# Out-projection products and gated sums of the prompt tiles placed inside the sample-attention loop

## The reference, cut to what matters

```python
def merge_out(attn, pool, ga, gb, w_att_out, w_pool_out, w_out):
    return (jax.nn.sigmoid(ga) * (attn @ w_att_out) + jax.nn.sigmoid(gb) * (pool @ w_pool_out)) @ w_out
...
o = jnp.einsum('bthk,btkd->bthd', p, v_sel)
...
mix_p = merge_out(attn_p, pool_p, ga, gb, w_att_out[i], w_pool_out[i], w_out[i])
...
mix_s = merge_out(attn_s, pool_s, gas, gbs, w_att_out[i], w_pool_out[i], w_out[i])
```

## Time and profile before

| | |
|---|---|
| time, median of 3 runs | 1365.29 us (1365.12 to 1371.73) |
| the profiled execution | 1370.32 us, span 1368.7 us, mean granted TensorE clock 0.957 |
| PE busy | 1239.2 us, 91% of the span |
| DVE, ACT, POOL busy | 645.3, 231.0, 470.7 us |
| DMA | 318.65 MB, mean 233 GB/s |

### The profile page before, as it was taken

One profiled execution on the slowest core, in us unless ns is written; L12 is line 12 of the kernel. 1 busy time (PEld: TensorE's weight loads), 2 busy tenths in 40 slices (PEclk: granted clock), 3 DMA queues, 4 the chain that ended last, 5 costly groups with the idle time before them and its releaser, 6 DMA issues. The chain is left out here.

```text
span 1368.7 us, 20749 instructions
## 1 busy us (share of the span) xinstructions
PE 1239.2 (91%) x7495; PEld 519.1 (38%) x7495; DVE 645.3 (47%) x1110; ACT 231.0 (17%) x496; POOL 470.7 (34%) x586
## 2 busy tenths in 40 slices
PE   5999889999999799998899899898999998988896
PEld 3555443445545534554332222222222222223342
DVE  1336579969972533783332323223232232321894
ACT  1124331022233410010011111011110110111210
POOL 5444516212243000254444344444344343430022
PEclk9999989999999999999899999999999999999998
DMA  8233220122111266032689999999999999997851
GB/s 278 63 123 95 62 77 9 62 77 86 24 24 25 78 231 261 32 144 100 232 319 413 402 407 415 416 390 415 395 414 402 400 410 383 416 384 290 369 154 38
DMA packets 97754, 318.65 MB, mean 233 GB/s; under 512 B 51737, under 2 KB 53533, under 8 KB 80120
## 3 DMA queue, kind: packets, MB, share of 16 engines
q1 hardware_dynamic: 74992, 273.11, 51.8%
q0 software_dynamic: 22672, 44.30, 8.8%
HBM read 298.70 MB, written 31.33 MB: 241 GB/s over the span
## 5 line engine op out<-in xcount | busy, mean ns | idle before, releaser
L1659 PE MATMUL ps<-arena 128*32 128x512 f32 x3072 | 356.9, 618 | 44.7 <-DMA arena<-in_w_exp 42.2
L2135 DVE STREAM_TRANSPOSE arena<-arena 128x1024 f32<-128x1024 f32 x48 | 100.0, 2084 | 260.7 <-DMA arena<-h_rows,arena 260.7
L983 POOL DMA_INDIRECT arena<-h_rows,arena x192 | 193.3, 1007 | 76.5 <-issue 75.6
L1659 PEld LDWEIGHTS ps<-arena 128*32 128x32 f32 x3072 | 97.9, 114 | 267.6 <-issue 215.4
L1672 PE MATMUL ps<-arena 128*32 128x512 f32 x1536 | 173.5, 592 | 0.8 <-DVE arena L2169 0.8
L1319 PE MATMUL ps<-arena 128*128 128x512 f32 (+1 forms) x384 | 166.3, 591 | 4.9 <-DMA arena<-in_w_in 4.8
L1047 ACT ACTIVATE arena<-ps 128x512 f32<-128x512 f32 (+5 forms) x226 | 103.0, 486 | 367.4 <-PE ps L1295 198.9
L990 POOL DMA_INDIRECT y_rows<-arena x48 | 48.8, 1017 | 300.8 <-DVE arena L2169 290.0
L1319 PEld LDWEIGHTS ps<-arena 128*128 128x128 f32 x384 | 72.5, 191 | 91.3 <-issue 90.6
L1672 PEld LDWEIGHTS ps<-arena 128*32 128x32 f32 x1536 | 49.5, 110 | 115.6 <-issue 115.6
L1250 ACT ACTIVATE arena<-ps 128x256 f32<-128x256 f32 x48 | 18.4, 384 | 387.7 <-PE ps L1659 387.7
(11 more groups left out here) (230 smaller groups left out, 1332.1 us busy)
## 6 DMA issues: line engine op xcount, KB each, us to landing
arena<-in_w_exp SPq DMA_DIRECT2D x64, 2048.0 KB, 20.2
arena<-in_w_exp SPq DMA_DIRECT2D x64, 1024.0 KB, 16.0
arena<-y_rows SPq DMA_DIRECT2D x8, 2048.0 KB, 8.6
arena<-in_w_in SPq DMA_DIRECT2D x6, 2048.0 KB, 7.9
arena<-in_x_prompt SPq DMA_DIRECT2D x8, 512.0 KB, 9.6
arena<-in_cache_v SPq DMA_DIRECT2D x128, 32.0 KB, 1.7
arena<-in_w_out SPq DMA_DIRECT2D x2, 2048.0 KB, 12.1
arena<-in_w_ple_gate SPq DMA_DIRECT2D x2, 2048.0 KB, 17.3
```

The source lines that it names most:

```text
L983: pool.indirect_dma_start(out=xg[s][:, 256 * g:256 * g + 256], out_offset=None, in_=h_quarters, in_offset=bass.IndirectOffsetOnAxis(ap=fro ...
L1659: ins = mm(ps[e % 3][q, :], xgT[e % 2][:, kk, q], w13[slots[g]][:, kk, :], start=(kk == 0), stop=(kk == KT - 1))
L2135: v.transpose(xgT[e % 2].rearrange("p c (g i) -> p g c i", g=4), xg[e % 3].rearrange("p (g j c) -> p g c j", g=4, c=KT)).then_inc(turned, 1)
```

## The change

The job list puts `m1` of prompt tile `p` (both halves) into step `p`, between `ps` and `ost`:

```diff
         for i in range(5):
             add(("ps", p, i), "act" if i % 2 else "dve")
+        add(("m1", p, 0), "dve")
+        add(("m1", p, 1), "dve")
         add(("ost", p), "dve")
-    for t in range(4):
-        for c in range(2):
-            add(("m1", t, c), "dve")
     add(("m1", 4, 1), "dve")
```

ACT's sigmoids of the first gate move from behind the four exponentials to the place ahead of them:

```diff
             att_copy(3)
+            for t in range(NT):
+                r = ROWS[t]
+                nc.scalar.activation(sga[0:r, t, :], sga[0:r, t, :], ACT.Sigmoid).then_inc(gate_a_ready, 1)
 
             for p in range(4):
                 act.wait_ge(maxed, 32 + p + 1)
...
-            for t in range(NT):
-                r = ROWS[t]
-                nc.scalar.activation(sga[0:r, t, :], sga[0:r, t, :], ACT.Sigmoid).then_inc(gate_a_ready, 1)
```

PE makes the first half's products between the transposes and the values' products of a step, the second half's between these and the turn of the result:

```diff
+            def attention_out(t, c):
+                w = weights(pe, "wao")
+                key = ("m1", t, c)
+                if t == 4:
+                    fills(in_halves(claim(pe, key), attnT, w, 512, 4), key)
+                    return
+                b = claim(pe, key)
+                for k in range(4):
+                    ins = mm(b[:, :], attnT[:, k, span(t)], w[:, k, 512 * c:512 * c + 512], start=(k == 0), stop=(k == 3))
+                fills(ins, key)
...
                 turn4(("ps", p, 4), [logit[:, p, PAST:SK]], P, DT)
+                attention_out(p, 0)
                 for i in range(5):
                     read(pe, ("ps", p, i))
...
                 ins.then_inc(pv_done, 1)
+                attention_out(p, 1)
                 pe.wait_ge(att_ready, p + 1)
                 turn4(("ost", p), [attS], P, HD)
 
-            w = weights(pe, "wao")
             read(pe, ("ost", 3))
-            for t in range(4):
-                for c in range(2):
-                    key = ("m1", t, c)
...
-            fills(in_halves(claim(pe, ("m1", 4, 1)), attnT, w, 512, 4), ("m1", 4, 1))
+            attention_out(4, 1)
```

DVE's gated sum becomes a function `merge`, called twice in each step, ahead of the copy of `ost`:

```diff
+            def merge(t, c, b):
...
+                ins = v.tensor_tensor(m[0:r, t, cs], m[0:r, t, cs], tmp, ALU.add)
+                if c == 1:
+                    ins.then_inc(m_ready, 1)
...
+                dve.wait_ge(gate_a_ready, p + 1)
+                merge(p, 0, take(dve, ("m1", p, 0)))
                 dve.wait_ge(expd, 32 + p + 1)
...
                 v.tensor_scalar(attS, ps[6 + p % 2][:, 0:HD], erec[:, p:p + 1], None, ALU.mult).then_inc(att_ready, 1)
+                merge(p, 1, take(dve, ("m1", p, 1)))
                 key = ("ost", p)
```

More of the change, by code:

```diff
@@ L1963, in bias_max @@
                 v.tensor_scalar(nmax[:, p:p + 1], mx[:, 0:1], -1.0, None, ALU.mult).then_inc(maxed, 1)
+            def merge(t, c, b):
+                r, cs, tmp = ROWS[t], slice(512 * c, 512 * c + 512), mtmp[c][0:ROWS[t], :]
+                key = ("m1", t, c if t < 4 else 1)
+                if t == 4 and c == 0:
+                    link(v.tensor_tensor(tmp, b[0:NS, :], sga[0:r, t, cs], ALU.mult))
+                else:
+                    rows = b[:, :] if t < 4 else b[NS:P, :]
+                    frees(v.tensor_tensor(tmp, rows, sga[0:r, t, cs], ALU.mult), key)
+                    mine(key)
+                ins = v.tensor_tensor(m[0:r, t, cs], m[0:r, t, cs], tmp, ALU.add)
+                if c == 1:
+                    ins.then_inc(m_ready, 1)
             dve.wait_ge(expd, 32)
+            dve.wait_ge(mixed, 2 * NT)
             bias_max(0)
@@ L1986, in _ @@
                 frees(ins, key)
[L1989 to L2009, removed]
+            dve.wait_ge(gate_a_ready, NT)
+            b = take(dve, ("m1", 4, 1))
+            for c in range(2):
+                merge(4, c, b)
             for t in range(NT):
```

## The result

The changed kernel is slower: 1392.78 us median (1392.48 to 1393.71), the kernel before, run beside it, 1367.54 (1365.12 to 1371.73); ratio 1.0169, 95% interval 1.0141 to 1.0196. The forecast was 1388.5 in a range of 1378 to 1396.

A forecast was written before the change was run, and what follows sets the result against it. SP's load queue decides: late `w_att_out` 16.3, slow first half 3.46 + 2.0, other halves 24.2 − 3.46, gaps −4.5 make 38.0; less `w_out`'s 17 spare, plus 2.0 slow start, 23.2. Forecast 1388.5, range 1378 to 1396.

The forecast's parts named there:

- The wait for `w_att_out`: Ahead of the first out-projection products: PE idles 10 to 13 until this load lands at 469.8.
- Slow starts: PE's first out-projection products and first `w_out` products, after long idles, each take 2.0 longer; bounds 0 and 2.0.
- The row that the forecast held against the slow start: Values' products in the earlier trace that took the usual 2.08 after a gap of 1.89.
- Steps: Attention steps 1 to 3: 14.1 a step, DVE's 4.8 holding PE partly idle; bounds 13.1 and 16.1.
- the 4.5 that the sum took off for gaps: PE gaps in the attention steps won on balance, subtracted in the 38.0 delay of the last values' products.
- `w_out`: Load complete 23.7 after the last values' products, at 541.2; PE idles 6.5, its products start 21.2 late.
- Carried one to one: Behind the `w_out` products, loads, stores and waits hang together as before, so the whole delay carries on.
- rival 4: Delay swallowed by the experts: 23 of their 42.2 of weight waits could vanish; 1365, chance 0.04.
- Rivals 1 and 2: `w_out` comes in time: 14.6 late, 1379.9, chance 0.13; `w_att_out` comes in time: 11.4 late, 1376.7, chance 0.04.
- Rival 3: Products fill the attention steps' 10.2 of gaps, lengthening nothing; `w_out` products start 2.8 earlier: 1362.5, chance 0.03.

The follow-up runs named there:

- e1: Changed kernel with `w_att_out` issued ahead of the last sequence's cached values instead of behind them; 1376.07 us, ratio 1.0047 to the kernel before.
- e8: Changed kernel with the first gate's five sigmoids moved behind the second exponential, both loads left late; 1392.25 us, ratio 1.0170 to the kernel before.
- e4: Changed kernel with residual rows, norm weights and router weights issued after step 1's values' products; 1384.95 us, ratio 1.0108 to the kernel before.
- e6: Changed kernel with `w_att_out` and residual rows issued earlier, sigmoids behind the second exponential, bias products and maximum inside the preceding step; 1359.43 us, ratio 0.9943.
- e7: Kernel before with `w_att_out`, residual rows and norm weights issued earlier, as a control; 1367.56 us, ratio 1.0000.

## Why the prediction was right, step by step

- **The wait for `w_att_out`** was the first step and came as described: 11.95 of idle (10 to 13 forecast), ended by that load. It landed at 472.5 in place of 469.8, since SP issued it 2.5 later in this execution; e1 shows that the wait is a cost, e8 that it covers the sigmoids. Its size is partly luck: the same list up to these products waited 15.92 in e4, because there PE was further ahead of SP. The earlier trace rows was also read for more than it shows: the row of cached values begins where its view does (50 loads, 1.34 each), while SP issues 96 of them in one run from 332.30. Only the end of that row went into the sum.
- **Slow starts** were put at 2.0 each and measured 1.5 (5.16 against 3.67 to 3.70) and 1.6 (29.28 against 27.70). The granted clock, a share of full speed, shows two levels: of the 2784 half microseconds of the changed kernel 2452 stand at 1.00 and 286 at 0.50, the other 46 between them, and in the kernel before 2482, 213 and 42 of 2737. In the idle it was 0.50 (470.00 to 472.47), and 0.70 over the first products: 0.50 up to 475.00 and 1.00 from 475.50. Over the first products with `w_out` it was 0.50 from 543.94 to 547.00. The bound of 2.0 was too low: in e1 the products with `w_out` start 3.0 slow (30.70, clock 0.50 from 526.89 to 531.00), in e4 the first half (6.66, clock 0.55). The row that the forecast held against the slow start has an idle of 1.89; the two slow starts measured here stand behind 11.95 and 7.63, so it was no test of idles as long as these.
- **Steps** were put at 14.1 and take 14.2. The lower bound of 13.1 for PE's own work was too high: e6 runs a step in 12.5. From the start of the stretch the last values' products end 37.4 later than before, where 38.0 was forecast; the 4.5 that the sum took off for gaps is a balance of these times and has no row of its own.
- **`w_out`** was put at 23.7 behind the last values' products; it is there 24.0 behind them (527.17 + 16.6 from issue to landing, against 519.81). The idle was 7.63 for 6.5 forecast: that left out the 0.56 that PE waits there for ACT, and the turn of `m` began 59.5 after the first product, not 59.9. In e4, where the residual rows and norm weights come ahead of both halves, each half lands in 7.7 to 7.8.
- **Carried one to one:** the stretch lost 21.0, the products behind it 1.6, 22.6 in all, and the two executions entered it 2.9 apart for reasons ahead of the change. That makes 25.5, but the spans differ by 23.3: 2.2 were won back later on. The waits for expert weights are 39.7 against 42.2, 2.5 less, so the experts swallowed at most little, and rival 4, which needs all 23, is out. (The 2.5 may be no effect at all: these waits are 36.9 in e7, which has PE's list of the kernel before.) That 23.3 falls on the forecast's 23.2 is therefore chance: it holds an entry 2.9 late and 2.2 won back, neither of them in the sum; the part that the sum describes is 22.6. The medians differ by 25.2.
- **The median** came out 4.3 above the forecast; 2.3 of this is the kernel before, whose median rose from 1365.29 to 1367.54 with a fourth run; the other 2.0 is open.
- **Rivals 1 and 2** are what e4 and e1 bring about: 14.6 and 11.4 were worked out for them, and 10.8 thousandths (about 15) and 4.7 thousandths (about 6, by the medians 8) measured; the second was too high. **Rival 3's** bound, that even full gaps could give no more than 2.8 because `w_out` follows the last values' products, holds only as long as the residual rows are loaded between them: e6, which moves these and fills the gaps, wins 6.6 by the medians.

## What to carry to other kernels

Before products are put into an engine's waiting time, follow their operands back to the queue that loads them: here the weights were issued behind 64 small loads, 1.34 each, and were on time only because they were used late. Then look at what starts on the end of the stretch that is being lengthened; a load that had 17 to spare was late once its trigger moved by 40. And a gap is filled for free only if the other engine's answer to the new work does not stand ahead of the work that ended the gap.

## What the runs showed that I had not expected

Equal idle did not bring equal clocks. Ahead of the turn of `m` PE idles 3.00 in every kernel here. The 40 transposes behind it take 4.36 in the kernel before and in the changed one, at a granted clock of 1.00, 6.03 in e1, at 0.72, and in the control e7, at 0.59:

```profile
471.55 3.68 PE L1529 MATMUL ps<-arena 128*64 128x64 f32 x64 [0.74 <-ACT arena L1049]
...
516.97 7.22 PE L1297 MATMUL ps<-arena 128*128 128x128 f32 x40 [3.00 <-DVE arena L2009]
```

From 512 to 525 the granted clock is 1.00 in the kernel before and 0.74 in e7, whose PE list is the same; its stretch is 79.1 against 73.3, and its time is the same (ratio 1.0000). Behind the two long waits of the change the products start at a granted clock of 0.50 (472.47 to 475.00 and 543.94 to 547.00); behind the short gaps they go either way in these executions. What decides it is not shown: each kernel has one trace. So of one profiled execution a difference of some 5 in this stretch says little; the idles and what ends them say more.

ACT's table load at the router's first sigmoid did not wait with the activation behind it. In the changed kernel's ACT timeline this load and the one at the first exponential, 1.28 each, begin at most 0.03 after the instruction ahead of them ends, and the router's is over 0.79 before its activation starts:

```profile
448.31 4.84 ACT L1190 ACTIVATE arena<-arena 128x1024 f32<-128x1024 f32 x5
453.18 1.28 ACT L1194 ACT_TABLE_LOAD   x1
454.47 2.01 ACT L1194 ACTIVATE arena<-arena 128x2056 f32<-128x2056 f32 x1
...
573.69 1.09 ACT L1046 ACTIVATE arena<-ps 128x512 f32<-128x512 f32 x2 [37.22 <-PE ps L1294]
574.79 1.28 ACT L1213 ACT_TABLE_LOAD   x1
576.86 0.22 ACT L1213 ACTIVATE arena<-ps 128x64 f32<-128x64 f32 x1 [0.79 <-PE ps L1569]
```

At the router the load ends 0.79 before PE's products, and costs nothing, as the forecast had it. At the exponential, whose maximum ended at 449.85, nothing covers it but PE's wait for `w_att_out`.
